# A spatial gate moved between the S5 input products of a hybrid gMLP / S5 / attention kernel

## The reference, cut to what matters

```python
def _chunk_gmlp(u, v, v_g, w_s, b_s):
    v = _layer_norm(v, v_g)
    vc = v.reshape(Bn, L // CHUNK, CHUNK, A_GROUPS, A_GROUP_W)          # chunks of 128 tokens, 4 groups of 128
    mixed = jnp.einsum('gpq,bnqgc->bnpgc', w_s, vc) + b_s.T[None, None, :, :, None]
    return u * mixed.reshape(Bn, L, A_WIDTH)
...
u, v, g_a, xs, g_b = jnp.split(h @ w_in, [...], axis=-1)
fwd = _s5_direction(xf, ...)      # bu = einsum('blgh,gph->blgp', u, bb): the state's input
bwd = _s5_direction(bwd_seq, ...)
```

## Time and profile before

| | |
|---|---|
| time, median of 3 runs | 1251.14 us (1249.95 to 1252.96) |
| time of the profiled execution | 1251.19 us |
| span in the profile | 1249.4 us |
| TensorE busy | 1193.1 us, 95% of the span |
| VectorE busy | 801.8 us, 64% |
| ScalarE busy | 510.7 us, 41% |
| mean granted TensorE clock | 0.991 |

### The profile page before, as it was taken

The page is one execution under the profiler, slowest core; times in us unless marked ns, Lnnn a source line. Parts: engine busy times, 40 slices in busy tenths (PEclk is TensorE's granted clock), DMA queues, the critical chain, the costliest instruction groups (busy, mean ns, idle before and its releaser), DMA issues.

```text
span 1249.4 us, 17213 instructions
## 1 busy us (share of the span) xinstructions
PE 1193.1 (95%) x6722; PEld 981.2 (79%) x6722; DVE 801.8 (64%) x1264; ACT 510.7 (41%) x945; POOL 465.2 (37%) x347
## 2 busy tenths in 40 slices
PE   3899999999999999999999999988999999999997
PEld 2777789888889858877888878876788888887885
DVE  5698849899725172157559792169777777765127
ACT  3445446110025241145233431266666666665012
POOL 4700000000000003423112111259999999999232
PEclk9899999999999999999999999999999999999999
DMA  9935776326412942222022113220000000000313
GB/s 341 338 110 169 205 221 221 118 106 236 153 51 98 366 160 54 68 102 101 1 68 68 34 60 118 76 84 9 18 9 18 9 18 9 18 9 10 135 34 135
DMA packets 81025, 129.85 MB, mean 104 GB/s; under 512 B 12945, under 2 KB 43025, under 8 KB 80145
## 3 DMA queue, kind: packets, MB, share of 16 engines
q1 hardware_dynamic: 71120, 113.96, 27.2%
q10 hardware_dynamic: 9824, 14.80, 3.4%
HBM read 97.81 MB, written 30.93 MB: 103 GB/s over the span
## 4 chain that ended last, share of the span: by engine, by line
PE 77%; DVE 11%; DMA 5%; POOL 3%; ACT 2%; issue 1%; SPq 0%; ACTq 0%; POOLq 0%; DVEq 0%
PE ps L1794 8%; PE ps L1796 8%; PE ps L1795 8%; PE ps L1805 5%; PE ps L1806 5%; PE ps L1807 5%; DVE region_d L1071 3%; PE ps L2075 3%; PE ps L2109 3%; PE ps L2110 3%; PE ps L2111 3%; PE ps L2095 3%; PE ps L2098 3%; PE ps L2097 3%; PE ps L2096 3%; PE ps L1656 2%
## 5 line engine op out<-in xcount | busy, mean ns | idle before, releaser
L656 POOL TENSOR_TENSOR region_b<-region_b,region_d 128x512 f32<-128x512 f32 x20 | 26.3, 1327 | 477.7 <-DVE region_d L1465 477.7
L1794 PE MATMUL ps<-w_hi,a_hi 128*128 128x512 f32 x448 | 177.7, 397 | 4.5 <-DVE b_lo L1159 3.9
L1795 PE MATMUL ps<-w_lo,a_hi 128*128 128x512 f32 x448 | 175.3, 391 | 0.0
L1561 DVE TENSOR_REDUCE small<-ps 128x1 f32<-128x1280 f32 x64 | 95.3, 1489 | 75.6 <-PE ps L2075 75.6
L1796 PE MATMUL ps<-w_hi,c_lo 128*128 128x512 f32 x368 | 143.3, 389 | 0.0
L649 POOL TENSOR_TENSOR w_lo<-weight_ring,w_hi 128x2048 fp32r<-128x2048 f32 x15 | 69.5, 4631 | 190.8 <-ACT w_hi L707 190.8
L1805 PE MATMUL ps<-a_hi,w_hi 128*128 128x512 f32 (+1 forms) x384 | 138.0, 359 | 0.0
L1806 PE MATMUL ps<-b_lo,w_hi 128*128 128x512 f32 (+1 forms) x384 | 136.0, 354 | 0.0
L1807 PE MATMUL ps<-a_hi,w_lo 128*128 128x512 f32 (+1 forms) x384 | 135.9, 354 | 0.0
L680 POOL TENSOR_TENSOR region_c<-region_c 128x512 f32<-128x512 f32 x80 | 128.6, 1608 | 16.3 <-ACT region_c L1046 12.0
L1794 PEld LDWEIGHTS ps<-w_hi,a_hi 128*128 128x128 f32 x448 | 84.8, 189 | 24.0 <-issue 5.6
(11 more groups left out here) (234 smaller groups left out, 2729.3 us busy)
## 6 DMA issues: line engine op xcount, KB each, us to landing
weight_ring<-in_w_mod SPq DMA_DIRECT2D x10, 2048.0 KB, 9.2
weight_ring<-in_we_in SPq DMA_DIRECT2D x10, 1024.0 KB, 5.7
weight_ring<-in_wo_in SPq DMA_DIRECT2D x10, 1024.0 KB, 5.1
weight_ring<-cop_t_scratch SPq DMA_DIRECT2D x4, 1536.0 KB, 7.8
region_c<-in_w_mod SPq DMA_DIRECT2D x2, 2048.0 KB, 21.4
bop_scratch<-region_d ACTq DMA_DIRECT2D x16, 256.0 KB, 2.6
cop_t_scratch<-region_d SPq DMA_DIRECT2D x8, 512.0 KB, 7.6
weight_ring<-bop_scratch SPq DMA_DIRECT2D x2, 2048.0 KB, 10.2
```

The costliest lines, as they stand in the source:

```text
L1561: v.tensor_reduce(smax[:, i % 2, h:h + 1], ps[:, 0:3, :].rearrange("p b n -> p (b n)")[:, 0:TOK], AX.X, ALU.max).then_inc(s_a_max, 1)
L1794: te.matmul(o, th, wh[:, k % 4], start=k == 0, stop=False)
L1795: te.matmul(o, th, wl[:, k % 4], start=False, stop=False)
```

## The change

The gate's 10 tiles are split into three groups. Tiles 0 to 2 run after step 9 of the `xs` product, tiles 3 to 6 after step 10, and tiles 7 to 9 in the middle of step 11, between its first four and its last four blocks of the contraction. They use banks 2, 3 and 6 in turn in place of 4 and 5. Each tile waits for its own chunk of `v`, and from the fourth tile on for the tile three before it to be taken out. The wait for the copy-out of all 12 `xs` steps ahead of the gate is gone. The third block-operator product, the first to write bank 2, waits until VectorE has taken out all ten gate tiles.

```diff
+        GMB = (2, 3, 6)
...
-                    last = v.scalar_tensor_tensor(out=vt[:, t, fs], in0=ps[:, 4 + t % 2, fs], scalar=vgain[:, g:g + 1], in1=bsb[:, fs],
+                    last = v.scalar_tensor_tensor(out=vt[:, t, fs], in0=ps[:, GMB[t % 3], fs], scalar=vgain[:, g:g + 1], in1=bsb[:, fs],
...
+            def spatial_gate(tiles):
+
+                if tiles[0] == 0:
+                    pe.wait_ge(s_ws_ev, 1)
+                    pe.wait_ge(s_bl_ev, 16)
+                for t in tiles:
+                    pe.wait_ge(s_vg_ok, t + 1)
+                    if t >= 3:
+                        pe.wait_ge(s_gm_ok, t - 2)
+                    for g in range(FB):
+                        last = te.matmul(ps[:, GMB[t % 3], P * g:P * g + P], vt[:, t, P * g:P * g + P], wsT[:, g], start=True, stop=True)
+                    last.then_inc(s_gm_mm, 1)
...
-                f_part(j, "xs", XB[j % 3]).then_inc(s_xs_mm, 1)
+                if j < 11:
+                    f_part(j, "xs", XB[j % 3]).then_inc(s_xs_mm, 1)
+                else:
+                    f_part(j, "xs", XB[j % 3], range(4))
+                    spatial_gate(range(7, TT))
+                    f_part(j, "xs", XB[j % 3], range(4, KT)).then_inc(s_xs_mm, 1)
                 between_tiles(after_xs.get(j, ()))
-
-            pe.wait_ge(s_ws_ev, 1)
-            pe.wait_ge(s_vg_ok, TT)
-            pe.wait_ge(s_xs_ev, 12)
-            for t in range(TT):
-                if t >= 2:
-                    pe.wait_ge(s_gm_ok, t - 1)
-                for g in range(FB):
-                    last = te.matmul(ps[:, 4 + t % 2, P * g:P * g + P], vt[:, t, P * g:P * g + P], wsT[:, g], start=True, stop=True)
-                last.then_inc(s_gm_mm, 1)
+                if j in (9, 10):
+                    spatial_gate(range(3) if j == 9 else range(3, 7))
...
+                if j == 2:
+                    pe.wait_ge(s_gm_ok, TT)
```

## The result

The changed kernel took 1257.8 us (median of 8 runs, 1256.1 to 1261.8) against 1253.3 us for the kernel before on the same chip (8 runs, 1250.0 to 1255.6). The ratio is 1.0041, with a 95% interval of 1.0029 to 1.0054, which is 5.1 us (the two medians lie 4.5 us apart). The change makes the kernel slower, by more than the 0.2% that can be told from no change. The profiled execution took 1257.74 us around a span of 1255.9 us, 6.5 us more than the span before; that profiled execution of the kernel before was 2.2 us faster than the median of its 8, so the two spans alone overstate the change.

What follows compares the result with a forecast made beforehand. The chain was taken to run through copy-out, `xs_scratch` store and `bop` 1 load, not the gate. Gate 9.7 less 7.3 us gave +2.4, the clock +2.2: 1251.19 to 1255.8 us, 8-in-10 range 1252.0 to 1258.5.

Steps and rivals of the forecast that it cites:

- The gate ahead of the product's end: All 80 gate records precede the `xs` product's end on TensorE and delay it by 9.7 us (9.3 to 11.6).
- The gate fits between the products: Between the `xs` products, chunks of `v` and VectorE keep up, and the third block-operator product's wait costs nothing.
- Now `bop` 0 is still issued at 180.5 us: The `bop` 0 load keeps its issue time and is out of the store's way at about 190 us.
- The store's price alone: Fourth block's 640 KB store to `xs_scratch`, without `bop` 0 beside it: 4.6 us in place of 11.9, at least 3.0.
- The clock's 2.2 us on the path: Idle time ahead of the block-operator products' second half lowers TensorE's clock, and that half loses 2.2 us (1.7 to 2.8).
- The sum: Whole run: 1251.19 us plus 2.4 for the second half's later start plus 2.2 for the clock, 1255.8 us.
- the load of `bop` 1: Issued when the store has landed, with the `U` load beside it as before: 9.9 us.
- The store does not get quicker: Rival, chance 0.06: short pieces keep the `xs_scratch` store at 9 to 11.9 us; about 1261 us or more.
- The gate does not fit: Rival, chance 0.09: TensorE waits between products for `v` or VectorE, the gate costs 11.6 us; 1257.7 us.
- not slower: Rival, chance 0.05: TensorE's own saving of 3.4 us by the second half becomes the chain; 1247.8 us.
- The clock holds: Rival, chance 0.2: no lower clock in the second half, only its later start counts; 1253.6 us.
- The shift behind is one constant: Sign: everything behind the second half shifts by one constant; wrong if the shift is given back behind 215 us.

Runs made afterwards that it cites:

- the kernel with the cut `bop` 0: The changed kernel with only 64 KB of `bop` 0 loaded, the first 16 products using that piece; ratio 1.0005 against the kernel before.
- the kernel with the banks alone: The kernel before with the gate still behind step 11 but in banks 2, 3 and 6, without the copy-out wait; ratio 1.0005.
- the last kernel: Changed kernel's gate, fourth `xs` block staged in `shared`, ring slots 0 and 2 swapped, read-back on SyncE behind `bop` 1; 0.9983 against the kernel before.
- the filled kernel: The changed kernel plus 36 products that nobody reads behind step 11; ratio 1.0042 against the kernel before.
- the fourth kernel of the cut link: Changed kernel's gate, fourth `xs` block staged in `shared` in two pieces, ring slots 0 and 2 swapped; ratio 1.0059 against the kernel before.

## Why the prediction was right in number and wrong in two steps

**The gate ahead of the product's end: right.** 9.7 us were forecast and 8.98 measured. A record takes 0.111 us, (3.73 - 0.275) / 31, where I had 0.116, and 80 of them 8.9 us. The four changes of mode, for which I allowed 0.4 us, cost under 0.1.

**The gate fits between the products: right.** No idle time in its three groups; VectorE was done in time, and the wait of the third block-operator product for it was hidden.

**"Now `bop` 0 is still issued at 180.5 us": wrong, and this is the step that failed.** It was issued at 190.15 us. I had read its issue time off the trace as if it were given by SyncE's own queue, since no wait stood before it. It stood at a wait for the `xs` product too, through the ring slot, and that wait happened to be over. The store term was to fall from 11.9 to 4.6 us and fell to 9.73, 5.1 us more than forecast; the second half came 6.5 us later and not 2.4.

**The store's price alone, 4.6 us: too high.** It is 3.66 us, between my lower bound of 3.0 and the 4.6. With `bop` 0 out of the way the shift is 0.3 us (33.9 against 33.61), which the kernel with the cut `bop` 0 shows. No run has the whole `bop` 0 loaded early and the store alone behind it. By these numbers such a kernel would lose some 0.3 us, and 1.7 us more where the clock fell in the longer idle time, which is an estimate from the second half at low clock (10.63 against 8.96 us). Had the premise on `bop` 0 been right, the loss would then have been some 0.3 to 2.0 us, less than a run can tell, and not 4.6. The Trainium skill's fit in DMA: Bandwidth & Descriptors, "Anatomy of one DMA", gave an estimate of 3.5 us for it, and the trace with the cut `bop` 0 agrees (3.66), though the fit was made on another issue path. For a load of 2048 KB the same fit gives 6.8 us, an estimate, and rows 11 have 9.4; there the measurement decides.

**The clock's 2.2 us on the path: wrong.** The idle time came ahead of the first half, since that half's operand was late, and the low clock was over at 203.3 us, before the second half. Filling the gap kept the clock up and gained no time. The rule that I drew from the rows, that an idle time of this length lowers the clock, was right; the place followed from the step that failed.

**The sum.** The start of the second half was 4.1 us off (6.5 - 2.4): +5.1 for the store, -0.7 for the gate (8.98 against 9.7) and -0.3 for the load of `bop` 1. The clock's 2.2 us on the path were not there. That leaves +6.5 against the +4.6 forecast, which is what the two profiled spans show; the runs show +5.1. So the number agrees by luck, two errors against each other. Of the prediction's own signs most failed: the store was to take 4 to 6 us, TensorE to stand idle 5 to 6 us ahead of the second half (0.26), and that half to take 10.5 to 12 us (8.96).

**The rivals.** "The store does not get quicker" had the right effect for the wrong reason and 0.06 of the chance: its 9 to 11.9 us were put down to short pieces, and the run without company shows 3.66. "The gate does not fit" and "not slower" are refuted. "The clock holds" is refuted as said, but what it was to lead to, no low clock on the path, came true.

**The shift behind is one constant: nearly.** The `gb` products begin 7.5 us later in absolute time (they start at 218.90 against 211.41 us), of which 1.0 us was there at step 9. The spans differ by 6.5 us. Some 1 us is given back between 584 and 756 us, where attention begins: SyncE's load issue of 576.51 us before comes 7.4 us later, the one of 749.60 us 6.5. What gives it back was not tried.

## What to carry to other kernels

Before a product is delayed, list everything that waits for its end, in the program and not in the trace: the copy-out, the store behind it, and each load whose ring slot the product's own weights occupy. A wait that is already over when an engine reaches it leaves no row, and becomes real when its condition moves.

Work that fills a transfer's wait cost nothing here, and it stops being free when it is moved ahead of what issues the transfer: ten tiles cost nothing behind the product and 0.90 us each in front of it, less what the store gave back.

When a transfer is given more company to take it off one engine's path, look for its other waiters. Freeing `bop` 1 alone lost 0.4%; with the read-back moved as well, so that ScalarE waits for nothing, the same cut gained 0.2%.

## What the hardware showed that I had not expected

- One store of 640 KB from ring to memory took 3.66 us alone, 6.3 beside small stores, 9.6 to 10.1 beside one load of 2048 KB, 11.9 to 12.2 beside that load and the small stores, and 16.1 beside two loads, though its bytes are a third of one load's. It landed 1.9 us after the load it started with (200.51 against 198.65 us; before, 192.73 against 191.0, 1.7 us). That agrees with what the Trainium skill says in DMA: Bandwidth & Descriptors, "Queues, rings and completion order": each DMA engine takes turns between the queues that have work, a packet at a time. These runs show the totals and not the turns.
- TensorE's clock fell 3.0 us after its last matmul in the changed kernel, in a gap of 8.66 us. In the kernel with the banks alone it fell 2.2 us after it, just behind a gap of 2.06 us, and it fell behind a gap of 1.94 us in the last kernel. It held through gaps of 1.71 us (the filled kernel) and 1.88 us (the kernel with the cut `bop` 0), and through one of 2.12 us ahead of the first half in the fourth kernel of the cut link, whose clock reads 1.00 in each us from 192 to 197. So near 2 us the length of the gap alone did not decide it in these runs. Where it fell at a gap on the path it cost 1.7 and 1.8 us.
